# Rotary scores of the decode attention: one float32 product against three products of high and low parts

## The reference

```
def mla_softmax(qn, qp, kn, kp, v, mask):
    s = jnp.einsum('bqhd,bkhd->bhqk', qn, kn) + jnp.einsum('bqhd,bkd->bhqk', qp, kp)
    s = jnp.where(mask, s.astype(jnp.float32) * MLA_SCALE, NEG_INF)
    pr = jax.nn.softmax(s, axis=-1).astype(v.dtype)
    return jnp.einsum('bhqk,bkhd->bqhd', pr, v)
```

## Time and profile before

| | |
|---|---|
| median of three runs | 1338.93 us |
| the profiled execution: its own time, and its span | 1340.77 us, 1338.9 us |
| PE busy, PEld busy | 1245.5 us (93%), 1140.1 us (85%) |
| DVE, ACT, POOL busy | 725.4 us (54%), 531.7 us (40%), 448.4 us (33%) |
| granted clock of PE over the span | 0.974 of 2.4 GHz |
| instructions | 26519 |

### The profile page before, as it was taken

The page is one execution under the profiler, slowest core; times in us unless marked ns, Lnnn a source line. Parts: engine busy times, 40 slices in busy tenths (PEclk is TensorE's granted clock), DMA queues, the critical chain, the costliest instruction groups (busy, mean ns, idle before and its releaser), DMA issues.

```text
span 1338.9 us, 26519 instructions
## 1 busy us (share of the span) xinstructions
PE 1245.5 (93%) x8624; PEld 1140.1 (85%) x8624; DVE 725.4 (54%) x1318; ACT 531.7 (40%) x1378; POOL 448.4 (33%) x632
## 2 busy tenths in 40 slices
PE   4999999998999999969859999999999999999698
PEld 4999985678999999958859999867789999999588
DVE  4455655664566555645244555556646556655451
ACT  4222135344555555524042121353445555555230
POOL 1023045423554445420020330454334445544200
PEclk9999999999999999989969999999999999999799
DMA  9421113003523223303513320220135222222035
GB/s 313 159 101 57 44 50 100 1 21 103 177 72 79 74 74 78 80 1 126 180 55 101 101 77 24 66 84 1 31 102 170 78 79 76 75 72 74 1 120 187
DMA packets 132780, 115.95 MB, mean 87 GB/s; under 512 B 46513, under 2 KB 127346, under 8 KB 132658
## 3 DMA queue, kind: packets, MB, share of 16 engines
q1 hardware_dynamic: 132658, 114.52, 28.7%
HBM read 103.56 MB, written 13.27 MB: 87 GB/s over the span
## 4 chain that ended last, share of the span: by engine, by line
PE 42%; issue 28%; POOL 17%; POOLq 7%; DVE 3%; ACT 2%; DVEq 1%; DMA 0%; SPq 0%; ACTq 0%
POOL krs L2170 15%; PE ps L543 7%; PE ps L544 7%; PE ps L545 7%; PE ps L637 3%; POOLq L2164 3%; POOLq L2166 2%; PE ps L551 2%; PE ps L552 2%; POOL rstat L2005 2%; PE ps L793 1%; PE ps L816 1%; PE ps L794 1%; PE ps L650 1%; POOLq L2000 1%
## 5 line engine op out<-in xcount | busy, mean ns | idle before, releaser
L1860 DVE TENSOR_REDUCE kss<-ksq 128x8 f32<-128x1024 f32 x128 | 156.0, 1219 | 216.7 <-ACT ksq L1386 216.7
L543 PE MATMUL ps<-w_hi,hT_hi 128*128 128x408 f32 (+2 forms) x704 | 243.3, 346 | 0.1
L544 PE MATMUL ps<-w_lo,hT_hi 128*128 128x408 f32 (+2 forms) x704 | 241.4, 343 | 0.0
L545 PE MATMUL ps<-w_hi,hT_lo 128*128 128x408 f32 (+2 forms) x704 | 240.7, 342 | 0.0
L1386 ACT ACTIVATE ksq<-ps 128x544 f32<-128x544 f32 x256 | 160.1, 625 | 199.7 <-PE ps L964 199.7
L964 PE MATMUL ps<-wq_hi,cT_hi 128*128 128x272 f32 x1024 | 223.3, 299 | 0.0
L2170 POOL TENSOR_TENSOR krs<-kss_t,cst 128x8 f32<-128x8 f32 x128 | 209.5, 1636 | 19.0 <-DVE Ssc L1874 2.5
L964 PE MATMUL ps<-wq_lo,cT_hi 128*128 128x272 f32 x1024 | 212.5, 289 | 0.0
L964 PE MATMUL ps<-wq_hi,cT_lo 128*128 128x272 f32 x1024 | 212.2, 289 | 0.0
L964 PEld LDWEIGHTS ps<-wq_lo,cT_hi 128*128 128x128 f32 x1024 | 161.9, 190 | 0.0
L964 PEld LDWEIGHTS ps<-wq_hi,cT_lo 128*128 128x128 f32 x1024 | 161.5, 189 | 0.0
(11 more groups left out here) (196 smaller groups left out, 2017.7 us busy)
## 6 DMA issues: line engine op xcount, KB each, us to landing
ckv<-in_cache_ckv SPq DMA_DIRECT2D x256, 128.0 KB, 2.0
raw<-in_w_in SPq DMA_DIRECT2D x68, 408.0 KB, 4.0
kp<-in_cache_kpe SPq DMA_DIRECT2D x256, 32.0 KB, 1.8
raw<-in_w_out SPq DMA_DIRECT2D x16, 340.0 KB, 3.8
S<-in_state_ret SPq DMA_DIRECT2D x8, 512.0 KB, 5.9
out<-S SPq DMA_DIRECT2D x8, 512.0 KB, 3.2
z<-out SPq DMA_DIRECT2D x2, 2048.0 KB, 8.5
wqb<-in_w_qb SPq DMA_DIRECT2D x3, 1152.0 KB, 9.7
```

The costliest lines, as they stand in the source:

```text
L543: pe.matmul(out, a_hi, b_hi, start=first, stop=False)
L544: pe.matmul(out, a_hi, b_lo, start=False, stop=False)
L545: return pe.matmul(out, a_lo, b_hi, start=False, stop=last)
L1860: dve.tensor_reduce(kss[:, hs, 2 * k:2 * k + 2, :], ksq[:, q % 2, :, c0:c0 + HW].rearrange("p j (h k) -> p j h k", h=H), AX.X, ALU.add).th ...
```

## The change

The rotary queries are split once per layer, by DVE at the start of stage 2, into float32r high parts `qp_hi` and low parts `qp_lo` (the low parts over `qp_s` itself). ACT's copy of the turned rotary keys becomes their high part, and DVE makes their low part right behind `cT_lo`. The one float32 matmul becomes three float32r matmuls of 64 columns through the helper `product` (rows L545 to L547 of the new kernel), and PE waits for DVE's low part (`kpT_lo_ok`) where it waited for ACT's copy (`kpT_ok`). The new `kpT` holds both parts and lies over weights that the stage doesn't need.

```diff
     qt32 = place("qt32", [P, KC, NB, H, NT], FP32, at)
+    qp_hi = nc.alloc_sbuf_tensor_at("qp_hi", [P, NB, 2, H, NT], FP32R, offset=A0)
...
+    qp_lo = nc.alloc_sbuf_tensor_at("qp_lo", [P, NB, 2, H, NT], FP32R, offset=at[0])
     qp_s = place("qp_s", [P, NB, 2, H, NT], FP32, at)
...
-    kpT = place("kpT", [P, 2, P], FP32, at)
+    kpT = nc.alloc_sbuf_tensor_at("kpT", [P, 2, 2, P], FP32R, offset=NORM_AT)
...
                 if not first:
-                    pe.wait_ge(kpT_ok, n)
+                    pe.wait_ge(kpT_lo_ok, n)
                 pe.transpose(ps[:, 5, 0:P], kp[b][:, 2 * q:2 * q + 2, :].rearrange("p n k -> p (n k)"), ident)\
                     .then_inc(kp_turned, 1)
...
-                pe.wait_ge(kpT_ok, n + 1)
-                pe.matmul(ps[:, 6, 0:2 * HQ], kpT[:, par, :],
-                          qp_s[:, bass.ds(seq, 1), :, :, :].rearrange("p b j h q -> p (b j h q)"),
-                          start=True, stop=True).then_inc(rp_ps, 1)
+                pe.wait_ge(kpT_lo_ok, n + 1)
+                out = ps[:, 6, 0:2 * HQ]
+                w_h, w_l = (w[:, bass.ds(seq, 1), :, :, :].rearrange("p b j h q -> p (b j h q)") for w in (qp_hi, qp_lo))
+                product(out, (kpT[:, par, 0, :], kpT[:, par, 1, :]), (w_h, w_l), True, True).then_inc(rp_ps, 1)
...
                 act.wait_ge(kp_turned, n + 1)
-                act.activation(kpT[:, par, :], ps[:, 5, 0:P], ACT.Copy).then_inc(kpT_ok, 1)
+                act.activation(kpT[:, par, 0, :], ps[:, 5, 0:P], ACT.Copy).then_inc(kpT_ok, 1)
...
                                   ALU.subtract).then_inc(c_lo_ok, 1)
+                dve.wait_ge(kpT_ok, n + 1)
+                dve.tensor_tensor(kpT[:, par, 1, :], ps[:, 5, 0:P], kpT[:, par, 0, :].bitcast(FP32), ALU.subtract)\
+                    .then_inc(kpT_lo_ok, 1)
...
+            dve.tensor_copy(qp_all[0], qp_f)
+            dve.drain()
+            dve.tensor_tensor(qp_all[1], qp_f, qp_all[0].bitcast(FP32), ALU.subtract)
+            dve.drain()
             beside_w(0, 0)
             keep_pair(0, 0, True)
```

More of the change, by code:

```diff
@@ L322, in build @@
          "attn_probs_kept", "attn_out_in_psum", "attn_y_ready"))
-    c_turned, c_hi_ok, c_lo_ok, kp_turned, kpT_ok, kk_ps, kk_sq, kk_kept, kk_ss, kk_rs = (sem(n) for n in
-        ("page_latents_turned", "page_hi_kept", "page_lo_kept", "page_kpe_turned", "page_kpe_kept",
+    c_turned, c_hi_ok, c_lo_ok, kp_turned, kpT_ok, kpT_lo_ok, kk_ps, kk_sq, kk_kept, kk_ss, kk_rs = (sem(n) for n in
+        ("page_latents_turned", "page_hi_kept", "page_lo_kept", "page_kpe_turned", "page_kpe_hi_kept", "page_kpe_lo_kept",
          "page_keys_in_psum", "page_keys_squared", "page_scores_kept", "page_keys_summed", "page_inv_root"))
@@ L1942, in sequence @@
                         beside_w(seq + 1, 1 - b)
+            qp_all = (qp_hi[:, :, :, :, :].rearrange("p b j h q -> p (b j h q)"),
+                      qp_lo[:, :, :, :, :].rearrange("p b j h q -> p (b j h q)"))
+            qp_f = qp_s[:, :, :, :, :].rearrange("p b j h q -> p (b j h q)")
+            dve.tensor_copy(qp_all[0], qp_f)
+            dve.drain()
+            dve.tensor_tensor(qp_all[1], qp_f, qp_all[0].bitcast(FP32), ALU.subtract)
+            dve.drain()
             beside_w(0, 0)
```

## The result

The changed kernel takes 1352.98 us (median of four runs, 1350.24 to 1353.96) against 1338.72 us for the kernel before in the same comparison. The ratio is 1.009, with a 95% interval of 1.0069 to 1.011: it is slower by 9 to 15 us. The forecast was 1350.7 us, and the measured time lies in its range of 1343 to 1357 us.

A forecast was written before the change was run, and what follows sets the result against it. The prediction took PE to bound the kernel, busy some 269 of 276 us per decode stage. Exposed products, 10.8 us, plus the start, 1.0 us, gave +11.8 us on 1338.93: 1350.7 us, range 1343 to 1357.

The forecast's parts named there:

- PE's added load: Rotary product on PE: a third weight load with its matmul adds 0.11 us, from 0.16 to 0.27 us per pair.
- 98 of 128 products count: Decode stages: 28 products hide in boundary waits, 2 behind layers' last pairs; 98 exposed products cost 10.8 us.
- the slack: PE's wait for DVE before turning the maximum at sequence boundaries: 0.62 us, said to swallow 2 x 0.11.
- DVE's low part at nothing: DVE's added low part of `kpT` per pair: no cost, bound 4 us if all came onto the path at boundaries.
- The split at the start: DVE's query split ahead of `beside_w`: 1.4 us, of which 0.88 idle, leaving 0.5 us, twice: 1.0 us.
- The sum: Whole kernel: 10.8 us for exposed products plus 1.0 us for the start, +11.8 us, slower by 0.9%.
- The signs that it named: Profile after: pair 3.84 us, PE's wait about 0.40, sequence +0.66, DVE +38, `cT_lo` 0.5 later, no PE wait for `kpT`'s low part.
- The rival of columns: Rotary product on PE: loads hide, columns decide, three products cost 0.09 us instead of 0.16; 1333.0 us, chance 0.07.
- The rival of a smaller loss: Rotary product on PE: third load partly overlaps the transposes' first load, half of 0.11 us added; 1345.3 us, chance 0.15.

The follow-up runs named there:

- a kernel with less wait: The changed kernel with DVE, after pair 0, doing the old sequence's half scores and maximum, then pair 2's `cT_lo`, before pair 0's sum: 1338.74 us, ratio 0.9986.
- the reordered kernel of before: The kernel before with DVE, after pair 0, doing the old sequence's half scores and maximum, then pair 2's `cT_lo`, before pair 0's sum: 1323.91 us, ratio 0.9878.

## Why the prediction was right

- **PE's added load, put at 0.11 us per product.** Shown as the cause: taking products away one by one takes 0.112 and 0.119 us each, doing the float32 product twice adds 0.22, halving the moving columns changes nothing, and float32 passes with half of the weight columns are 0.057 and not 0.111 us apart. The size was short: 0.133 us where transposes follow directly, 0.118 on average over the six exposed places. The trace of before had no float32r matmul of few columns, and the rows of float32 passes gave the load, but not the 0.02 us at the step to the transposes. (The 0.108 us from the earlier trace rows holds a first step of 0.06; by their loads it is 0.111.)
- **98 of 128 products count.** The boundary holds: two products cost 18 ns together there, and a kernel with less wait pays for one of them. The other is cheap there even with DVE ahead, 0.06 and 0.09 us, so that the slack is not its only reason. The last product of a layer is hidden, by the 4.58 us in both traces. 98 x 0.118 = 11.6 us, where the forecast had 10.8; the records have 12.1 from the last wide matmul of a layer's first pair to that of its last, since the sixteen products of the first sequence of each layer cost 0.136 us each, and the two products at each of the fourteen boundaries 18 ns together.
- **DVE's low part at nothing.** Shown, from both sides (1340.18 us with it alone, 1351.25 us without it).
- **The split at the start, 0.5 us per layer.** 0.30 us: the copy took 0.43 us and not the 0.6 that I had assumed. That makes 0.6 us in all and not 1.0.
- **The sum.** 11.6 + 0.6 = 12.2 us, in the middle of the measured interval of 9 to 15 us, and 11.8 were forecast. That this is so close is in part luck: the product was put too low by 0.8 to 1.3 us in all, and the start too high by 0.4. The two profiled executions differ by 13.1 us. From the first transposes of a decode stage to its last wide matmul the records have 275.18 and 275.16 us before, 281.34 and 281.56 after, which is 12.6 of them; the other 0.5 lie outside the decode stages. Single executions of one kernel differ by up to 4 us.
- **The signs that it named.** An ordinary pair is 3.865 us long (3.84 were forecast), PE's gap before the turn of the maximum is 385.76 - 385.10 - 0.27 = 0.39 us (0.40), a sequence grows by 0.73 us (0.66), and PE waits for the low part of `kpT` nowhere. `cT_lo` at the start comes 0.3 us later, counted from the first transposes (0.5), and DVE has 28 us more (38).
- **The rival of columns** fell with the run of 32 columns. The Trainium skill ("FP8 and Floating Point Precision", TensorE Precision Notes) counts four passes for a float32 product, from which three would be a gain. Here the float32 product shows as two loads with a matmul each, and costs as much as two float32r products save 0.02 us. The Trainium skill ("TensorE: Matmul & The Clock Gate", LDWEIGHTS) puts a load, in ns, at its columns over 1.2; for 128 columns that is an estimate of 107 ns. The runs come near it, with 112 to 119 ns per product.
- **The rival of a smaller loss**, a third load that overlaps with the transposes, was wrong in its sign: at that step the products lose 0.02 us and gain nothing.

## What to carry to other kernels

Count weight loads before columns: with a full stationary of 128 columns and a moving side of 64 or less, each matmul costs its load, and a float32 product is two of them, three split products are three. For so narrow a moving side, splitting float32 into high and low parts costs time. For a wide one the trace of before lets one estimate a gain, which no run here tries: two float32 passes of 512 columns (L794) start 0.43 us apart, so that a product of two takes 0.86 us or 0.0017 per column, while float32r matmuls of 408 columns (L543 to L545) start 0.19 us apart, so that three take 0.56 us or 0.0014 per column. And a wait of the bounding engine hides what is added in front of it: look there first for a gain, since here another order of DVE's work at that wait was worth more than the change cost.

## What had not been expected of the hardware

- The first of several narrow matmuls seems nearly free in the records (the second starts 0.03 us behind it, 416.59 and 416.62), and the time shows at the next ones and in the length of the transposes. Starts of single matmuls mislead; distances between like matmuls on either side don't.
- The step from narrow float32r matmuls to transposes costs 0.02 us more than that from float32 ones. Its mechanism stays open; only its place was tested.
- In the middle of wide float32r matmuls a narrow product is dearer than in front of the transposes (pairs of 3.780 against 3.733 us with the float32 product). In the records one more group of wide matmuls then lasts 0.50 us in place of 0.41.
- PE can still be held up where the profile reports no wait: in the reordered kernel of before the transposes start 0.05 us behind the end of `cT_lo`, and a longer product in front of them costs 18 ns, against 60 to 90 where DVE is 0.12 to 0.14 us ahead.
